# Second layer's norm: squares added a tile later, scaled tiles between the last updates, and the queries' operand in tiles of its own

## The chip, the cores and the metric

The program runs on one core of a Trainium2 chip. TensorE (PE) multiplies, VectorE (DVE), ScalarE (ACT) and GpSimd (POOL) work elementwise, SyncE (SP) issues the DMAs. Each has a queue of its own that runs in order; they meet through semaphores. The metric is device time in microseconds, the median of the runs.

## The reference

Two blocks on x of 1024 positions by 1024 features, in f32. The change lies in the second block, between its pooling layer and its windowed attention:

```python
x = x + gate * pool_mixer(...)               # x, the last product of the pooling layer
# keys and values, one head pair group
hk = modulate(rmsnorm(x, kv_norm_g), shift, scale);  kv = hk @ w_kv          # 1024 x 256
# queries and gates of the attention layer
h = modulate(rmsnorm(x, norm_g[1]), shift1, scale1); q, z = split(h @ w_in)  # 1024 x 2048
# then scores in a band of 128, softmax with sinks, values, silu(z), w_out, a last norm
def rmsnorm(x, g): return x * rsqrt(mean(x * x, axis=-1) + 1e-6) * g
```

Both norms need the same mean of squares of the finished x, with other gains and shifts.

## The kernel before

Everything is held transposed, features on partitions: x is eight tiles X0 to X7 of 128 features by 1024 positions, cut in two halves of 512 positions (h = 0, 1). Each f32 product is three fp32r matmuls of 512 columns (high by high, high by low, low by high), so a unit of 128 output features and one half costs 8 tiles times 3 = 24 matmuls. Operand tiles are `bh` (high) and `bl` (low); weights arrive by DMA in three raw tiles, ScalarE rounds them to `wh`, GpSimd subtracts to `wl`, each unit in two blocks, with six block slots.

The stage `keys` runs thus:

- TensorE makes the last product `pl` of the pooling layer, for h = 0 and then h = 1, tile by tile (12 matmuls each). VectorE adds each into X (`dve_update`), ScalarE squares the updated tile, and VectorE adds the square to an accumulator (`add_square`) right behind the update, so it waits for the square.
- When tile 7 of a half is added, `pe_sums` (eight small matmuls in the trace) sums over partitions, VectorE and ScalarE make the reciprocal root, VectorE spreads it on a diagonal, `pe_rstd` multiplies it out and ScalarE copies it as R (`act_rstd`).
- A pass scales the eight X tiles of one half: VectorE computes `tmp = X * g * R`, ScalarE adds the shift and writes `bh` (for odd tiles in two instructions), and the low part `bl` is made by VectorE for even tiles and by GpSimd for odd ones. Passes in order: 0 (keys, half 0), 1 (keys, half 1), 2 (queries, half 0), 3 (queries, half 1). Passes 2 and 3 write over the tiles of passes 0 and 1, so they wait for v2's product of that half. The scratch `tmp` has three halves (`sc`).
- Pass 0 stands behind the update of tile 2 of half 1; tiles 3 to 7 of half 1 are updated behind it.
- TensorE: k2 and v2 (keys and values) on half 0, then on half 1 (`pe_first_two`; sums of half 1 within k2 behind tile 5, rstd within v2 behind tile 1), then b0 and b1 (the first two of 16 units of queries and gates) likewise, then b2 to b15, both halves at once.
- ScalarE: pass 1, pass 2, then the copies of k2's result out of PSUM (kx0, kx1), of v2's (vt), weights of b1 and b2, then pass 3.
- SyncE: weight loads, the copy of kx between partitions, weight loads, the eight stores of X, then the stores of the queries.

PSUM is four tiles of two halves. `take` gives a wide request the tile whose halves were taken longest ago and a narrow one the half taken longest ago, and makes TensorE wait until the last owner is freed; k2's owner mark is freed by the copy kx1, v2's by vt.

In the attention `sp_window` loads the queries of head pair j; for j = 1 it first waits for `QZ`, the last product of b15.

The lines touched: `dve_scaled`, `act_scaled`, `pool_scaled` (L852 to L915), `dve_update` (L2060), `pe_keys` to `pool_keys` (L2831 to L3055), `sp_window` (L3119). The profile names helper lines: L67 is any matmul, L73 any ScalarE instruction, L76 and L79 VectorE and GpSimd instructions.

Of the kernel before, what the change touches and what calls it, by code (L numbers as in the profile page):

```python
# [133 lines left out]
class Norm:  # L134


    def __init__(self, name, X, acc, R, sq, dg, sc, acc2=None, g1=None, direct=False):
        self.direct = direct
        self.name, self.X, self.acc, self.R, self.acc2, self.g1 = name, X, acc, R, acc2, g1
        self.sq, self.dg, self.sc = sq, dg, sc  # L140
        self.two = g1 is not None
        self.passes = 0


class Net:
# [36 lines left out]
    def setup(self):  # L182
# [70 lines left out]
        self.bl = [m(f"bl{j}", 24 + j, FR) for j in range(NT)]  # L253
        gtile = [32, 33, 34, 35, 0, 1, 2, 3, 4, 5, 6, 7]
# [14 lines left out]
        self.kx0, self.kx1, self.vt = m("kx0", 4), m("kx1", 33), m("vt", 34)  # L269
# [4 lines left out]
        self.T2 = [m(f"t2{i}", 2 * i, cols=2048) for i in range(2)]  # L274
        self.pt2 = [(m(f"p2h{i}", 16 + i, FR), m(f"p2l{i}", 18 + i, FR)) for i in range(2)]
        self.qb = [(m(f"q2h{i}", (5, 20)[i], FR), m(f"q2l{i}", (6, 21)[i], FR)) for i in range(2)]
        otile = [24, 25, 26, 27, 28, 29, 30, 4, 31, 32, 35, 22, 23, 7, 33, 34]
# [3 lines left out]
        self.Y = [m(f"Y{j}", 16 + j if j < 6 else j - 6) for j in range(NT)]  # L281
# [19 lines left out]
        self.n4 = five("n4", self.X)  # L301
# [543 lines left out]
    def sc_place(self, nm, p, j):  # L845
        return 8 * p + j
# [5 lines left out]
    def dve_scaled(self, e, nm, p, h, g, lo, hi, shift=None, after=(), turned=False, hooks={}):  # L852

        c = slice(h * 512, h * 512 + 512)
        r = (nm.acc2 if nm.two else nm.R)[:, c]
        for j in range(NT + 1):
            if j < NT:
                i = self.sc_place(nm, p, j)
                s = nm.sc[i % len(nm.sc)]
                e.wait_ge(*self.at("r", nm.name, h, 1 if nm.two else 0))  # L860
                if i >= len(nm.sc):
                    e.wait_ge(*self.at("scfree", nm.name, i - len(nm.sc)))
                marks = [("scaled", nm.name, p, h, j)]
                if turned:
                    e.wait_ge(*self.at("copied", h, j))
                    marks.append(("free", ("xt", h, j)))
                x = self.ps(("xt", h, j)) if turned else nm.X[j][:, c]
                e.scalar_tensor_tensor(out=s, in0=x, scalar=g(j), in1=r, op0=ALU.mult, op1=ALU.mult).then_inc(
                    self.sig["vec"].up(*marks), 1)
            k = j - 1  # L870
            if k >= 0 and k % 2 == 0:
                i = self.sc_place(nm, p, k)
                s = nm.sc[i % len(nm.sc)]
                for event in after:
                    e.wait_ge(*self.at(*event))
                e.wait_ge(*self.at("scaled", nm.name, p, h, k))
                e.wait_ge(*self.at("nhi", nm.name, p, h, k))
                marks = ("nlo", nm.name, p, h, k), ("scfree", nm.name, i)
                if shift is None:
                    e.tensor_tensor(lo[k][:, c], s, hi[k][:, c].bitcast(F32), ALU.subtract).then_inc(  # L880
                        self.sig["vlo"].up(*marks), 1)
                else:
                    e.scalar_tensor_tensor(out=lo[k][:, c], in0=s, scalar=shift(k), in1=hi[k][:, c].bitcast(F32),
                                           op0=ALU.add, op1=ALU.subtract).then_inc(self.sig["vlo"].up(*marks), 1)
            if j in hooks:
                hooks[j]()

    def act_scaled(self, e, nm, p, h, hi, shift=None, after=(), hooks={}):
        c = slice(h * 512, h * 512 + 512)
        for j in range(NT):  # L890
            s = nm.sc[self.sc_place(nm, p, j) % len(nm.sc)]
            e.wait_ge(*self.at("scaled", nm.name, p, h, j))
            done = self.sig["ahi"].up
            if shift is not None and j % 2:
                e.activation(s, s, ACT.Identity, bias=shift(j)).then_inc(
                    self.sig["evac"].up(("shifted", nm.name, p, h, j)), 1)
                e.wait_ge(*self.at("shifted", nm.name, p, h, j))
            for event in after:
# [5 lines left out]
            if j in hooks:  # L904
                hooks[j]()

    def pool_scaled(self, e, nm, p, h, lo, hi, hooks={}):
        c = slice(h * 512, h * 512 + 512)
        for j in range(1, NT, 2):
# [1150 lines left out]
    def dve_update(self, e, nm, name, h, j, before, gate=None):  # L2060
# [12 lines left out]
        if not nm.two:  # L2073
            self.dve_square(e, nm, j, h)
# [756 lines left out]
    def pe_keys(self, e):  # L2831
        acts = self.made(*zip(*(self.GA[t] for t in range(12, 16))),
                         [[("ghi", "pool", t), ("glo", "pool", t)] for t in range(12, 16)])
        W = self.A["a_w_out_2"][0]
        self.pe_by_halves(e, "pl", lambda j: self.w8(W, 128 * j, 256, k0=1536, nk=4), acts, 4, 256,
                          {1: lambda: self.pe_sums(e, self.n4, 0), 2: lambda: self.pe_rstd(e, self.n4, 0)})
        self.pe_first_two(e, ("k2", "v2"), [self.w8(self.A["w_kv_2"], 128 * i) for i in range(2)], self.bh, self.bl,
                          self.n4, (0, 1))
        Wb = self.A["b_w_in_2"][0]
        self.pe_first_two(e, (("b", 0), ("b", 1)), [self.w8(Wb, 128 * i) for i in range(2)], self.bh, self.bl, self.n4,  # L2840
                          (2, 3), rstd=False)
        h = self.by_norm(self.n4, self.bh, self.bl, (2, 3))
# [7 lines left out]

    POOLED = ("prod", ("pool", 2, 7))
    POOL_OUT = ("prod", ("pl", 1, 7), 1)

    def sp_keys(self, e):
# [3 lines left out]
        e.wait_ge(*self.at("kx", 1))  # L2858
        e.dma_start(self.kx0[64:128, :], self.kx0[0:64, :]).then_inc(self.sig["kx0"].up(("kxt", 0)), 16)
        e.dma_start(self.kx1[0:64, :], self.kx1[64:128, :]).then_inc(self.sig["kx1"].up(("kxt", 1)), 16)  # L2860
        self.sp_w(e, ("b", 0))
        self.sp_w(e, ("b", 1))
        for j in range(NT):
            for h in (0, 1):
                e.wait_ge(*self.at("sum", "n4", h, j))
            e.dma_start(self.xs[j * 128:j * 128 + 128, :], self.X[j][:, :]).then_inc(
                self.sig[f"xs{j}"].up(("xs", j)), 16)
        for j in range(16):
            if j == 3:
                e.wait_ge(*self.at("gst"))  # L2870
                e.wait_ge(*self.at(*self.POOL_OUT))
# [34 lines left out]
    def act_keys(self, e):  # L2906
# [3 lines left out]
        def second():  # L2910
            self.act_rstd(e, self.n4, 0)
            self.act_scaled(e, self.n4, 0, 0, self.bh, self.md(48), [self.POOLED])

        self.half_units(e, "pl", 256, self.act_w,
                        lambda h, j: self.act_square(e, self.n4, j, h, ("sum", "n4", h, j)),
                        {1: lambda: self.act_sums(e, self.n4, 0), 2: second})
        self.act_w(e, "k2", 4)
        self.act_w(e, "v2", 4)
        self.act_sums(e, self.n4, 1)
        self.act_rstd(e, self.n4, 1)  # L2920
        self.act_scaled(e, self.n4, 1, 1, self.bh, self.md(48), [self.POOLED])
        self.act_scaled(e, self.n4, 2, 0, self.bh, self.md(24), [("prod", "v2", 0)])
        e.wait_ge(*self.at("prod", "k2"))
        e.wait_ge(*self.at(*self.POOL_OUT))
# [3 lines left out]
        e.wait_ge(*self.at("prod", "v2"))  # L2928
        e.activation(self.vt[:, :], self.ps("v2"), ACT.Copy).then_inc(self.sig["evac"].up(("vt",), ("free", "v2")), 1)
        self.act_w(e, ("b", 0), 4)  # L2930
        self.act_w(e, ("b", 1), 4)
        self.act_scaled(e, self.n4, 3, 1, self.bh, self.md(24), [("prod", "v2")])
# [60 lines left out]
    def dve_keys(self, e):  # L2993
        for event in self.POOL_TMP:
            e.wait_ge(*self.at(*event))
        self.half_units(e, "pl", 256, None,
                        lambda h, j: self.dve_update(e, self.n4, "pl", h, j, [("px", j, 2)], self.md(16)), {
            1: lambda: self.dve_sums(e, self.n4, 0),
            2: lambda: self.dve_scaled(e, self.n4, 0, 0, self.g3(2), self.bl, self.bh, self.md(48), [self.POOLED])})
        self.dve_sums(e, self.n4, 1)  # L3000
        self.dve_scaled(e, self.n4, 1, 1, self.g3(2), self.bl, self.bh, self.md(48), [self.POOLED])
        self.dve_scaled(e, self.n4, 2, 0, self.g3(1), self.bl, self.bh, self.md(24), [("prod", "v2", 0)])
        self.dve_scaled(e, self.n4, 3, 1, self.g3(1), self.bl, self.bh, self.md(24), [("prod", "v2")])
# [19 lines left out]
    def pool_keys(self, e):  # L3023
# [7 lines left out]
        self.pool_scaled(e, self.n4, 2, 0, self.bl, self.bh)  # L3031
        self.pool_w(e, ("b", 0), 4)
        self.pool_w(e, ("b", 1), 4)
        self.pool_scaled(e, self.n4, 3, 1, self.bl, self.bh)
# [84 lines left out]
    def sp_window(self, e):  # L3119
# [10 lines left out]
        def fetch(n):  # L3130
# [6 lines left out]
            if j == 1:  # L3137
                e.wait_ge(*self.at(*self.QZ))
            else:
# [381 lines left out]
```

## Time and profile before

| | us |
|---|---|
| median of 3 runs | 2616.27 (2615.64 to 2618.62) |
| the profiled execution, its time | 2616.37 |
| its span | 2614.1 |
| TensorE busy | 2491.4 (95%) |
| VectorE busy | 1665.0 (64%) |
| ScalarE, GpSimd busy | 950.2, 658.7 |

Times in the trace count from the span's start. The stage of the change lies between about 2095 and 2220 us, the units b2 to b15 run to 2380 us, the windowed attention to about 2505 us. The granted clock of TensorE over the span is 0.986.

### The profile page before, as it was taken

To read this page: it belongs to the slowest core of one execution; us is meant where nothing else is said; L and a number is where in the kernel's file an instruction comes from. 1 tells how busy PE (TensorE), PEld (TensorE's weight loads), DVE (VectorE), ACT (ScalarE), POOL (GpSimd) and SP (SyncE) were. 2 spreads that over 40 slices of the span, in tenths; PEclk is the share of its full clock that TensorE was granted. 3 is DMA by queue.
4 is the path that set the end of the run, shared out by engine and by line. 5 is a ranking of instruction groups with operands and counts; after the bars stand their busy time and mean duration, and the time that the engine had idled before them with its cause. 6 is when DMAs were issued, how large, how long until landed. Compare 5 with 4: busy or idle time off the path is not lost.

```text
span 2614.1 us, 32078 instructions
## 1 busy us (share of the span) xinstructions
PE 2491.4 (95%) x12208; PEld 2052.8 (79%) x12208; DVE 1665.0 (64%) x2829; ACT 950.2 (36%) x1764; POOL 658.7 (25%) x536
## 2 busy tenths in 40 slices
PE   7899999888999899999999999999999998999998
PEld 5688888777887688888888877888877775888987
DVE  4699999476425877786644368476595566104843
ACT  5521212577123422222312244233243245225842
POOL 3167322576443000000000120000000044334753
PEclk9999999999999999999999999999999999999999
DMA  5112333001354365564623132232355123533242
GB/s 187 33 41 65 97 97 112 26 1 67 127 189 125 105 199 188 171 188 141 231 75 113 61 109 81 97 97 89 105 201 217 43 70 113 177 118 104 102 159 100
DMA packets 264323, 302.10 MB, mean 116 GB/s; under 512 B 11272, under 2 KB 216556, under 8 KB 264172
## 3 DMA queue, kind: packets, MB, share of 16 engines
q1 hardware_dynamic: 263860, 299.96, 35.1%
q8 instruction: 99, 1.62, 0.3%
q14 instruction: 52, 0.43, 0.1%
q10 hardware_dynamic: 312, 0.09, 0.0%
HBM read 228.15 MB, written 70.29 MB: 114 GB/s over the span
## 4 chain that ended last, share of the span: by engine, by line
PE 83%; DVE 10%; ACT 4%; issue 1%; DMA 1%; POOL 1%; SPq 0%; DVEq 0%; ACTq 0%; POOLq 0%
PE ps L67 81%; PE ps L70 2%; DVE tmp L79 1%; DVE sm L79 1%; ACT tmp L73 1%; DVE tmp L76 1%; ACT pth L73 1%; DVE wl L76 1%; DVE X L79 1%; DVE pwa L76 1%; DVE B2l L76 1%; DVE ptl L79 0%; DVE bl L79 0%; DVE pwb L76 0%; DVE ws L76 0%
## 5 line engine op out<-in xcount | busy, mean ns | idle before, releaser
L76 POOL TENSOR_TENSOR wl<-raw,wh 128x512 fp32r<-128x512 f32 (+1 forms) x224 | 293.4, 1330 | 1568.6 <-ACT wh L73 1568.4
L73 ACT ACTIVATE wh<-raw 128x512 fp32r<-128x512 f32 (+1 forms) x388 | 226.4, 621 | 243.6 <-PE ps L67 183.3
L67 PE MATMUL ps<-B2h,wh 128*128 128x512 f32 x616 | 244.1, 396 | 13.5 <-DVE B2l L76 7.0
L67 PE MATMUL ps<-B2l,wh 128*128 128x512 f32 x616 | 241.3, 392 | 0.0
L67 PE MATMUL ps<-B2h,wl 128*128 128x512 f32 x616 | 241.1, 391 | 0.0
L73 ACT ACTIVATE tmp<-ps 128x512 f32<-128x512 f32 (+5 forms) x163 | 118.2, 736 | 325.2 <-PE ps L67 313.9
L76 DVE TENSOR_TENSOR tmp<-tmp,ps 128x512 f32<-128x512 f32 x204 | 138.4, 685 | 109.0 <-PE ps L67 92.7
L67 PE MATMUL ps<-ah,wh 128*128 128x512 f32 (+1 forms) x608 | 192.5, 393 | 9.2 <-DVE al L76 5.0
L73 ACT ACTIVATE wh<-ws 128x512 fp32r<-128x512 f32 x152 | 94.3, 626 | 291.4 <-DVE ws L76 263.9
L67 PE MATMUL ps<-B3h,wh 128*128 128x512 f32 x448 | 178.3, 398 | 15.2 <-DVE B3l L76 7.1
L67 PE MATMUL ps<-ah,wl 128*128 128x512 f32 (+1 forms) x608 | 190.4, 390 | 0.0
L67 PE MATMUL ps<-al,wh 128*128 128x512 f32 (+1 forms) x608 | 190.3, 390 | 0.0
L67 PE MATMUL ps<-B3l,wh 128*128 128x512 f32 x448 | 176.0, 393 | 0.0
L67 PE MATMUL ps<-B3h,wl 128*128 128x512 f32 x448 | 176.0, 393 | 0.0
L100 DVE MATCH_REPLACE8 sm<-m,sm 128x384 f32<-128x384 f32 (+2 forms) x192 | 167.9, 889 | 0.0
L97 DVE MAX8 m<-sm 128x8 f32<-128x384 f32 (+2 forms) x192 | 162.2, 893 | 0.0
L67 PEld LDWEIGHTS ps<-B2h,wh 128*128 128x128 f32 x616 | 116.4, 189 | 43.2 <-issue 8.0
L76 DVE TENSOR_TENSOR X<-X,ps 128x1024 f32<-128x1024 f32 (+1 forms) x56 | 59.6, 1068 | 132.1 <-PE ps L67 132.1
L67 PEld LDWEIGHTS ps<-ah,wh 128*128 128x128 f32 (+1 forms) x608 | 113.3, 187 | 36.5 <-issue 10.7
L67 PEld LDWEIGHTS ps<-B2h,wl 128*128 128x128 f32 x616 | 116.6, 189 | 24.8
L67 PEld LDWEIGHTS ps<-B2l,wh 128*128 128x128 f32 x616 | 116.7, 189 | 23.6 <-issue 0.2
L67 PEld LDWEIGHTS ps<-ah,wl 128*128 128x128 f32 (+1 forms) x608 | 113.6, 187 | 24.7 <-issue 0.2
(292 smaller groups left out, 5751.7 us busy)
## 6 DMA issues: line engine op xcount, KB each, us to landing
ada<-in_ada_w SPq DMA_DIRECT2D x48, 512.0 KB, 3.7
raw<-in_w_in SPq DMA_DIRECT2D x37, 512.0 KB, 4.4
raw<-in_a_w_in SPq DMA_DIRECT2D x33, 512.0 KB, 4.6
gates<-tmp SPq DMA_DIRECT2D x32, 512.0 KB, 3.0
raw<-in_w_ffn_gate SPq DMA_DIRECT2D x24, 512.0 KB, 5.9
hd<-tmp SPq DMA_DIRECT2D x22, 512.0 KB, 4.6
gf<-hd SPq DMA_DIRECT2D x22, 512.0 KB, 7.2
raw<-in_a_w_out SPq DMA_DIRECT2D x20, 512.0 KB, 3.4
```

Of the source, the lines that this page charges most:

```text
L67: return self.e.matmul(*a, **k) if self.e else Ins()
L70: return self.e.transpose(*a, **k) if self.e else Ins()
L73: return self.e.activation(*a, **k) if self.e else Ins()
L76: return self.e.tensor_tensor(*a, **k) if self.e else Ins()
L79: return self.e.scalar_tensor_tensor(*a, **k) if self.e else Ins()
L97: return self.e.max(*a, **k) if self.e else Ins()
L100: return self.e.match_replace(*a, **k) if self.e else Ins()
```

## The change

1. Squares of half 1 are added a tile later: `update(j)`, then the square of tile j - 1. The sums of half 0 are made behind `pl`'s tile 0 and the rstd behind tile 1 (before: 1 and 2). Pass 0 begins earlier, and the updates of tiles 2 to 6 stand between its scaled tiles.
2. The operand of passes 2 and 3 gets tiles of its own (`bh2`, `bl2`): six of each are free when `pl` is done, and only the last two, which lie on `bh0` to `bh3`, wait for v2's product of that half. Tiles 0 to 3 of pass 2 are made before pass 1, the rest behind it. A fourth scratch half comes in.
3. k2 and v2 on half 0: the sums of half 1 come within v2, behind its tile 0, and the rstd behind its tile 4.
4. ScalarE copies kx0, kx1 and vt behind pass 3, the weights of b2 behind them. SyncE stores X before it loads the weights of b3 and b4 and copies kx. Tables, kx, vt, the second pair of query tiles, o2 and Y change places, and the wait for `QZ` goes.

```diff
+    self.bh2 = [m(f"bh2{j}", i, FR) for j, i in enumerate((4, 5, 6, 7, 0, 1, 16, 17))]
+    self.bl2 = [m(f"bl2{j}", i, FR) for j, i in enumerate((32, 33, 34, 35, 2, 3, 18, 19))]
...
+    self.n4 = Norm("n4", self.X, t[0], t[1], half(t[2]), half(t[3])[:1], half(t[3])[1:] + half(t[4]) + half(t[0])[:1],
+                   order=[(p, j) for p, n in ((0, range(8)), (2, range(4)), (1, range(8)), (2, range(4, 8)), (3, range(8))) for j in n])
...                                                                            # pe_keys
-                          {1: lambda: self.pe_sums(e, self.n4, 0), 2: lambda: self.pe_rstd(e, self.n4, 0)})
-        self.pe_first_two(e, ("k2", "v2"), ...)
+                          {0: lambda: self.pe_sums(e, n4, 0), 1: lambda: self.pe_rstd(e, n4, 0)})
+        self.pe_halves_of_two(e, ("k2", "v2"), ...,
+                              ({}, {0: lambda: self.pe_sums(e, n4, 1), 4: lambda: self.pe_rstd(e, n4, 1)}))
...
+    def pe_halves_of_two(self, e, keys, w8s, acts, hooks=({}, {})):
+        us = [self.unit(k, w) for k, w in zip(keys, w8s)]
+        for i in range(2):
+            self.gemm(e, keys[i], us[i], acts, (0,), hooks=hooks[i], end=False)
+        for i in range(2):
+            self.gemm(e, keys[i], us[i], acts, (1,))
+    def b_place_free(self, h):
+        return lambda j: [self.POOL_OUT] if j < 6 else [("prod", "v2", 0), ("prod", "v2")][h:h + 1]
...                                                                            # act_keys
+        self.act_scaled(e, n4, 0, 0, self.bh, self.md(48), [self.POOLED],
+                        hooks={0: square(2), 2: square(3), 3: four, 5: square(5), 7: six})
+        sq1(1, 7)
+        b0 = self.act_steps(e, n4, 2, 0, self.bh2, self.md(24), tiles=self.b_place_free(0))
+        next(b0)
+        self.act_sums(e, n4, 1)
+        for j in range(1, 4):
+            next(b0)
+        self.act_rstd(e, n4, 1)
+        self.act_w(e, "v2", 4)
+        self.act_scaled(e, n4, 1, 1, self.bh, self.md(48), [self.POOLED])
+        for j in b0:
+            pass
+        self.act_w(e, ("b", 0), 4)
+        self.act_scaled(e, n4, 3, 1, self.bh2, self.md(24), tiles=self.b_place_free(1))
+        e.wait_ge(*self.at("prod", "v2"))
         ... kx0, kx1 (frees k2), vt (frees v2)
         self.act_w(e, ("b", 1), 4)
...                                                                            # dve_keys
+        def second(j):
+            update(1, j, False)
+            if j > 1:
+                self.dve_square(e, n4, j - 1, 1)
+        second(0)
+        self.dve_sums(e, n4, 0)
+        second(1)
+        self.dve_scaled(e, n4, 0, 0, self.g3(2), self.bl, self.bh, self.md(48), [self.POOLED],
+                        hooks={0: later(2), 2: later(3), 3: later(4), 5: later(5), 7: later(6)})
+        second(7)
...                                                                            # pool_keys
         self.pool_w(e, "k2", 4)
+        self.pool_scaled(e, self.n4, 2, 0, self.bl2, self.bh2, tiles=range(4))
         self.pool_w(e, "v2", 4)
         self.pool_scaled(e, self.n4, 1, 1, self.bl, self.bh)
+        self.pool_scaled(e, self.n4, 2, 0, self.bl2, self.bh2, tiles=range(4, 8))
         self.pool_w(e, ("b", 0), 4)
+        self.pool_scaled(e, self.n4, 3, 1, self.bl2, self.bh2)
         self.pool_w(e, ("b", 1), 4)
...                                                                            # sp_window
-            if j == 1:
-                e.wait_ge(*self.at(*self.QZ))
-            else:
+            if j > 1:
                 e.wait_ge(*self.at("prod", ("s2", 4 * j - 5)))
```

GpSimd makes pass 0's low parts before the weights of k2 and v2, in both versions.

## Rows read from the trace of the kernel before

**Rows 1.** The page, part 4: shares of the chain that ended last.

```profile
PE 83%; DVE 10%; ACT 4%; issue 1%; DMA 1%; POOL 1%; SPq 0%; DVEq 0%; ACTq 0%; POOLq 0%
```

**Rows 2.** Stretches: length, busy PE, PEld, DVE, ACT, POOL, granted clock, DMA share, GB/s.

```profile
2151.00:2155.00 4.00, 3.39 (x8) 2.77 (x9) 2.82 (x4) 1.73 (x4) 1.53 (x3) 0.50 0.29 81
...
2220.00:2300.00 80.00, 80.00 (x340) 63.60 (x339) 8.57 (x7) 20.98 (x28) 27.75 (x20) 1.00 0.50 165
```

**Rows 3.** TensorE in order: start us, us, operation, idle before and its releaser.

```profile
2129.10 0.95 PE L67 MATMUL ps<-ones,tmp 128*128 128x1 f32 x8
...
2133.22 1.13 PE L67 MATMUL ps<-tmp,ones 128*128 128x512 f32 x2 [0.29 <-DVE tmp L76]
...
2151.61 0.77 PE L67 MATMUL ps<-bh,wh 128*128 128x512 f32 x1 [3.62 <-ACT tmp L73]
...
2160.12 1.36 PE L67 MATMUL ps<-ones,tmp 128*128 128x1 f32 x8 [1.49 <-DVE tmp L76]
...
2198.68 0.77 PE L67 MATMUL ps<-bh,wh 128*128 128x512 f32 x1 [2.25 <-POOL wl L76]
...
2213.98 0.47 PE L67 MATMUL ps<-bh,wh 128*128 128x512 f32 x1 [1.16 <-POOL bl L76]
...
2220.18 0.62 PE L67 MATMUL ps<-bh,wh 128*128 128x512 f32 x2
```

**Rows 4.** VectorE's waits, 2129 to 2214 us: in total, times, longest.

```profile
DVE bl L79 <- ACT bh L73: 7.0, 10, 5.3
DVE tmp L79 <- ACT tmp L73: 5.8, 1, 5.8
DVE tmp L76 <- ACT tmp L73: 4.9, 7, 0.7
```

**Rows 5.** VectorE in order, columns as in rows 3.

```profile
2134.53 1.57 DVE L76 TENSOR_TENSOR tmp<-tmp,tmp 128x512 f32<-128x512 f32 x1 [0.70 <-ACT tmp L73]
...
2168.76 1.42 DVE L79 SCALAR_TENSOR_TENSOR tmp<-X,gs,tmp 128x512 f32<-128x512 f32 x2 [5.78 <-ACT tmp L73]
...
2175.70 1.47 DVE L79 SCALAR_TENSOR_TENSOR bl<-tmp,mod,bh 128x512 fp32r<-128x512 f32 x1 [0.20 <-ACT bh L73]
...
2180.41 2.45 DVE L79 SCALAR_TENSOR_TENSOR tmp<-X,gs,tmp 128x512 f32<-128x512 f32 x2
...
2192.83 1.40 DVE L79 SCALAR_TENSOR_TENSOR tmp<-X,gs,tmp 128x512 f32<-128x512 f32 x2
```

**Rows 6.** ScalarE in order, columns as in rows 3.

```profile
2168.12 0.60 ACT L73 ACTIVATE tmp<-ps 128x512 f32<-128x512 f32 x1 [6.21 <-PE ps L67]
...
2193.57 2.04 ACT L73 ACTIVATE kx<-ps 64x1024 f32<-64x1024 f32 x2
...
2211.86 0.63 ACT L73 ACTIVATE bh<-tmp 128x512 fp32r<-128x512 f32 x1
```

**Rows 7.** GpSimd in order, columns as in rows 3.

```profile
2149.68 2.79 POOL L76 TENSOR_TENSOR wl<-raw,wh 128x512 fp32r<-128x512 f32 x2
...
2159.93 2.50 POOL L76 TENSOR_TENSOR wl<-raw,wh 128x512 fp32r<-128x512 f32 x2 [2.47 <-ACT wh L73]
...
2175.01 1.61 POOL L76 TENSOR_TENSOR bl<-tmp,bh 128x512 fp32r<-128x512 f32 x1 [2.05 <-ACT bh L73]
...
2197.26 5.89 POOL L76 TENSOR_TENSOR wl<-raw,wh 128x512 fp32r<-128x512 f32 x4 [1.91 <-ACT wh L73]
```

**Rows 8.** SyncE and TensorE in order, around the stores of x and the attention's start.

```profile
2200.26 7.99 SPq L109 DMA_DIRECT2D xs<-X  x8
...
2379.84 0.61 PE L67 MATMUL ps<-bh,wl 128*128 128x512 f32 x2
...
2381.54 0.32 SPq L109 DMA_DIRECT2D qd<-tmp  x1
...
2382.44 0.66 SPq L109 DMA_DIRECT2D q2h<-qd  x1
...
2389.10 0.33 PE L67 MATMUL ps<-k2h,q2h 64*128 64x128 f32 x2 [3.39 <-DMA q2l<-qd]
```

More of the change, by code:

```diff
@@ L845, in sc_place, with dve_scaled, dve_steps @@
     def sc_place(self, nm, p, j):
-        return 8 * p + j
+        return nm.order.index((p, j)) if nm.order else 8 * p + j
     def lows(self, p, j, shift):
         return "plo" if j % 2 else "vlo"
-    def dve_scaled(self, e, nm, p, h, g, lo, hi, shift=None, after=(), turned=False, hooks={}):
+    def dve_scaled(self, *a, hooks={}, **k):
+        for j in self.dve_steps(*a, **k):
+            if j in hooks:
+                hooks[j]()
+    def dve_steps(self, e, nm, p, h, g, lo, hi, shift=None, after=(), turned=False, tiles=None):
         c = slice(h * 512, h * 512 + 512)
@@ L873, in dve_scaled @@
                 s = nm.sc[i % len(nm.sc)]
-                for event in after:
+                for event in tiles(k) if tiles else after:
                     e.wait_ge(*self.at(*event))
@@ L884, in dve_scaled, with act_scaled, act_steps @@
                                            op0=ALU.add, op1=ALU.subtract).then_inc(self.sig["vlo"].up(*marks), 1)
+            yield j
+    def act_scaled(self, *a, hooks={}, **k):
+        for j in self.act_steps(*a, **k):
             if j in hooks:
                 hooks[j]()
-    def act_scaled(self, e, nm, p, h, hi, shift=None, after=(), hooks={}):
+    def act_steps(self, e, nm, p, h, hi, shift=None, after=(), tiles=None):
         c = slice(h * 512, h * 512 + 512)
@@ L897, in act_scaled @@
                 e.wait_ge(*self.at("shifted", nm.name, p, h, j))
-            for event in after:
+            for event in tiles(j) if tiles else after:
                 e.wait_ge(*self.at(*event))
@@ L2072, in dve_update @@
                                    op1=ALU.add).then_inc(self.sig["vec"].up(*marks), 1)
-        if not nm.two:
+        if not nm.two and squares:
             self.dve_square(e, nm, j, h)
@@ L2995, in dve_keys @@
             e.wait_ge(*self.at(*event))
[L2996 to L3003, printed above, removed]
+        n4 = self.n4
+        update = lambda h, j, squares=True: self.dve_update(e, n4, "pl", h, j, [("px", j, 2)], self.md(16), squares=squares)
+        def second(j):
+            update(1, j, False)
+            if j > 1:
+                self.dve_square(e, n4, j - 1, 1)
+        later = lambda j: lambda: second(j)
+        for j in range(NT):
+            update(0, j)
+        second(0)
[4 more added lines that the diff above has]
+        second(7)
+        b0 = self.dve_steps(e, n4, 2, 0, self.g3(1), self.bl2, self.bh2, self.md(24), tiles=self.b_place_free(0))
+        next(b0)
+        self.dve_square(e, n4, 7, 1)
+        next(b0)
+        self.dve_sums(e, n4, 1)
+        for j in range(2, 4):
+            next(b0)
+        self.dve_scaled(e, n4, 1, 1, self.g3(2), self.bl, self.bh, self.md(48), [self.POOLED])
+        for j in b0:
+            pass
+        self.dve_scaled(e, n4, 3, 1, self.g3(1), self.bl2, self.bh2, self.md(24), tiles=self.b_place_free(1))
         for j in range(NT):
```

85 lines of the change are left out of this document (43 added, 42 removed).

## The prediction

> **What bounds the kernel now.** I read the chain that ended last first: TensorE holds 83% of it, VectorE 10% and ScalarE 4% [rows 1]. A change that only moves norm work can therefore win no more than the places where that chain leaves TensorE. Next I cut the stretch of the diff by time. From 2220 us to the start of the windowed attention TensorE is busy without a gap at the full clock [rows 2], so whatever the stage gains or loses by the end of unit b1 is handed on unchanged, and the ruler is the first matmul of unit b2, at 2220.18 us [rows 3]. Between 2148 and 2220 us TensorE stands still before k2 (3.62 us), before the second sums (1.49), before b1 (2.25) and tile by tile in between, and after the first it runs at the 1.2 GHz level for a while (granted clock 0.50) [rows 2, 3].
>
> VectorE's waits say why [rows 4]: 4.9 us for ScalarE's squares (0.7 each), 5.8 us for the copied rstd of the second half, 7.0 us for ScalarE's high parts, of which 5.3 is one wait, while ScalarE copied kx and vt [rows 6]. That is 17.7 us of idle VectorE in front of a stage that VectorE paces: eight scaled tiles take 11.65 and 12.42 us (first scaled tile at 2168.76, 2180.41, 2192.83) [rows 5], while the 48 matmuls that they feed take 10.9.
>
> Passes 0 and 1 are the keys' operand of half 0 and 1, passes 2 and 3 the queries'. One VectorE instruction costs 0.67 us (two start within 1.42) [rows 5]. One matmul costs 0.227 at the full clock (27 from 2213.98 to 2220.18, the first a little longer) and 0.43 at half (8 in 3.39) [rows 2, 3].
>
> **Window stage: nothing.** The diff drops SyncE's wait for the last product of b before it loads the second pair of queries. TensorE does lose 3.39 us there, for that very load. But SyncE stores b15's tile first, at 2381.54, which itself comes after that product's last matmul (2379.84), and issues the load at 2382.44 [rows 8]. The removed wait had been met over a microsecond earlier and the queue order is unchanged: gain 0. Bounds: 0, and 3.39 if the load did go out earlier. The moved tables and kx tiles only rename places, and SyncE's eight stores of x move ahead of the loads of b3's and b4's weights and of the kx copies; I cost them at nothing, since those weights are used only behind b2, over 40 us after the updates of x are done. If that cover were gone, it would cost the 8 us that the stores take on SyncE [rows 8].
>
> **Pass 0 and k2's start: +3.0 us.** The sums of half 0 move ahead by one product of 12 matmuls, 2.72 us, from 2129.10, and the rstd matmul from 2133.22 to about 2130.5 [rows 3]. With ScalarE's copy behind a square, R is there near 2132.2. But now VectorE adds one update and one square between the scaled tiles. From the product of tile 2 (2130.5 + 0.6 + 2.72 = 2133.8) to the last scaled tile stand 18 instructions, 12.1 us, and GpSimd's operations among them hold up four at about 1 us: the square's addition of 1.57 at 2134.53 instead of 0.69, the low part of 1.47 at 2175.70 beside GpSimd's 1.61 at 2175.01 [rows 5, 7]. The last scaled tile is then ready at 2149.9, about 3 us later than without the updates between. Behind it ScalarE shifts and copies (1.4), GpSimd makes that tile's low part (1.5) and only then, in its order, k2's first weight block (1.5, the pair at 2149.68 took 2.79 [rows 7]), and 0.4 later TensorE starts: 2154.7 against 2151.61 [rows 3] (whose row names the square that ended last; by the times it is this weight block), taken as +3.0. The stall that should go grows to 7 us, because GpSimd's queue was not reordered. Bounds: 0 (nothing held) and +4.
>
> **The second half's rstd: +1.5 us.** k2's first half is 24 matmuls, 13 of them at the low clock as now: 8.1 us, to 2162.7. Then v2's first tile (0.7), the sums (1.0; the eight small matmuls took 0.95 at 2129.10 and 1.36 at 2160.12 [rows 3]), mean, root, reciprocal and diagonal (1.5): 2165.9. TensorE no longer limits: ScalarE's copy of R now stands behind pass 2's tiles 1 to 3, of which tile 3 can be scaled only after the diagonal, once at 0.67 and once held at 1.7, then 1.4 to shift and copy and 0.6 for R itself: 2170.2, against 2168.72 before [rows 6]. VectorE still waits about 4 us for these sums. Bounds: -1 and +3.
>
> **Twenty tiles instead of twenty-four.** Behind R come pass 1 (8 tiles), the last 4 of pass 2 and pass 3 (8); only 4 tiles have moved ahead, and the 5.3 us wait is gone. Eight tiles are 12.0 us on the mean of the two rows, or 12.7 up to ScalarE's last copy (for pass 2 13.2, from 2180.41 to kx's copy at 2193.57, which is 0.7 more than its 12.42 [rows 5, 6]). But the low parts of b0, which GpSimd made at 2159.93 while VectorE stood idle [rows 5, 7], now fall into pass 1, and those of b1 into pass 3: four more held instructions, 4.0 us. With 0.5 for b1's high parts in ScalarE's queue: 2170.2 + 12.0 + 2.0 + 6.0 + 12.7 + 2.0 + 0.5 = 2205.4 for ScalarE's last copy, which was 2212.49 [rows 6]. So the norm ends 7.1 us earlier. Bounds of the four: 0 and 1.7 each (the four at 2197.26 took 5.89 us and beside them VectorE's instructions came every 1.74 [rows 7]).
>
> The Trainium skill, "SBUF — State Buffer", Who interferes with whom, says that a VectorE instruction with two SBUF inputs and a GpSimd instruction that reads SBUF shut each other out completely, and that one with a PSUM input goes free. By that rule additions of squares and scaled tiles are the held kind and the updates are not, and four full operations of GpSimd at their mean of 1.4 us would make 5.6 of my 4.0 and the time 2623.8 us; the row at 2175.70 shows half to two thirds of an operation, so the sum stays with it.
>
> **What the earlier end is worth: the new wait.** TensorE's tail was short: the last tile of pass 3 is wanted late, in b0's second half, and only 27 matmuls follow (6.2 us). In the changed kernel b1's first half is behind another event. PSUM tiles are given to the one whose halves were taken longest ago. With the new order of takes (sums 0 before product 1; k2, v2, sums 1, b0, b1), b1 again gets k2's tile, since sums 1 now comes later than k2. That tile is free when ScalarE has copied kx1. Before, the copies stood ahead of pass 3 (2193.57, two of 1.02 [rows 6]) and b1 started at 2198.68 for GpSimd's weights [rows 3]. Now they stand behind it. Queued behind the waiting b1 are b0's second half and b1's own. So b1 starts at 2205.4 + 2.0 + 0.3 = 2207.7, after b0's first half has ended near 2199 (pass 1 done near 2184, v2's half and b0's half 5.4 each, from k2's last tile, with its gaps: 2188 + 10.9): TensorE stands for over 8 us. Then 72 matmuls follow, 16.3 us, the first ten at 0.43 as in the rows after a standstill (2.0 more; bounds 1.3 and 2.6): 2226.0. Against 2220.18 this is +5.8 us.
>
> **Sum.** The profiled execution took 2616.37 us with a span of 2614.1, 0.1 above the median of 2616.27, so both serve as base: 2616.4 + 5.8 = 2622.2 us. In parts, against before: up to the second R +1.5 (k2 starts 3.0 later, and the 1.49 standstill before its sums is gone); from R to ScalarE's last copy 35.2 us instead of 43.8, -8.6 (four tiles ahead -6.0, the one wait -5.3, held instructions and b1's high parts +4.5, and -1.8 for the crowd of held instructions that now follows that wait); from the last copy to b2 20.6 us instead of 7.7, +12.9.
>
> **Rivals.**
> A, the wait exists but decides less. The held instructions don't add up (0 instead of 4.0) and k2 starts at 2151.61: b1 starts at 2207.7 - 4.0 - 3.0 = 2200.7, the time is 2615.2. For it: 18 instructions that wait for nothing would leave GpSimd gaps. Against: rows 5 show three to four held of every twelve.
> B, the other side: b1 gets a tile that is free, and starts right behind b0. Then the stage ends by TensorE's own work or by pass 3's last tile: 2205.4 + 1.5 + 6.2 = 2213.1, -7.1 us, 2609.3 us. It decides if sums 1 is taken before v2 or if b0's tile is the later one; the order of takes in the diff speaks against it, the 17.7 us of idle VectorE for a gain as such.
> C, the removed wait of SyncE does release the load: 3.4 us less, 2618.8. Rows 8 speak against it.
> D, the norm is later than summed (second rstd after 2173, every block of weights held fully): b1 at 2212, 2627 us.
>
> **How the numbers follow.** Forecast 0.62 (2619 to 2626), A 0.16, B 0.10, C 0.04, D 0.08. About 0.2%, 5.2 us, is what a measurement tells from no change. The forecast lies just beyond it, so of its 0.62 some 0.44 is slower and 0.18 within; D is slower; A and C are within; of B 0.08 is faster and 0.02 within. Slower 0.53, same 0.39, faster 0.08. The range is 2615 to 2627: B is left out, and the two bounds of the held instructions and of k2's start (about -6 and +5 on the forecast) are in.
>
> **What would show it.** In the changed profile: k2's first matmul after an idle stretch of 6 to 8 us, with GpSimd's weights as releaser; the copy of the second R near 2170; a wait of TensorE of 6 to 9 us before b1, ended by ScalarE's kx copy (the surest sign); VectorE's wait for squares gone; pass 3's last copy on ScalarE near 2205; the 3.39 us wait for the second queries still there. The prediction is wrong if b1 starts right behind b0, or if b2 starts before 2218 us.

## The result, and the profile after

| | before | after |
|---|---|---|
| median of 6 runs each, us | 2616.11 (2614.26 to 2618.62) | 2626.14 (2623.30 to 2627.87) |
| the profiled execution, its span | 2614.1 | 2625.6 |

The changed kernel takes 1.0037 of the time before, 95% interval 1.0024 to 1.0050. A second series beside other kernels gave 1.0025 (1.0015 to 1.0035), 2624.52 against 2618.63 us. So it is slower by 6 to 10 us; forecast were 2622.2 (+5.8), with 2615 to 2627 as the range.

**How far apart the two traces stand where.** Below, the stage is counted from its own entry, the first 512-column update of X's second half: 2126.58 us before, 2131.41 after.

| from the entry, us | before | after | difference | forecast |
|---|---|---|---|---|
| k2's first matmul | 25.03 | 28.33 | +3.30 | +3.0 |
| second copy of R | 41.54 | 43.24 | +1.70 | +1.5 |
| ScalarE's last copy of pass 3 ends | 85.91 | 79.36 | -6.55 | -7.1 |
| b2's first matmul | 93.60 | 99.59 | +5.99 | +5.8 |
| b15's store, the end of the stage | 254.96 | 260.97 | +6.01 | +5.8 |

From that store to the end of the span it is 232.6 and 233.2 us. The other 4.83 us of the difference between the two spans lie ahead of the entry, where the kernels are alike; experiment 9 is about them. A "low clock" below is the 1.2 GHz level of TensorE.

TensorE in order in the changed kernel, as [rows 3]:

```profile
2131.21 0.95 PE L67 MATMUL ps<-ones,tmp 128*128 128x1 f32 x8
...
2135.34 1.12 PE L67 MATMUL ps<-tmp,ones 128*128 128x512 f32 x2 [0.29 <-DVE tmp L76]
...
2159.74 0.76 PE L67 MATMUL ps<-bh,wh 128*128 128x512 f32 x1 [6.91 <-POOL wl L76]
...
2168.64 0.95 PE L67 MATMUL ps<-ones,tmp 128*128 128x1 f32 x8
...
2180.14 0.77 PE L67 MATMUL ps<-bh,wh 128*128 128x512 f32 x1 [4.71 <-DVE bl L79]
...
2212.78 0.80 PE L67 MATMUL ps<-bh,wh 128*128 128x512 f32 x1 [8.86 <-ACT kx L73]
...
2231.00 0.62 PE L67 MATMUL ps<-bh,wh 128*128 128x512 f32 x2
```

Three stalls have taken the place of the old ones. The first, before k2, grew from 3.62 to 6.91 us and now names GpSimd's low weights. The second, 4.71 us ahead of the second halves of k2 and v2, is new: there TensorE waits for pass 1's first tile, which VectorE can only begin when it has the second R. The third, before b1, is new too: 8.86 us, ended by ScalarE's kx copy. The standstill before the second sums (1.49 in [rows 3]) is gone. The prediction speaks of the first and the third. The second costs nothing in this kernel, since b1 waits for the kx copy whatever TensorE does before; it counts once b1 has a tile of its own (experiment 8).

ScalarE in order, as [rows 6]: the second R, the last copy of pass 3, and right behind it the two kx copies.

```profile
2174.65 0.58 ACT L73 ACTIVATE tmp<-ps 128x512 f32<-128x512 f32 x1
...
2210.14 0.63 ACT L73 ACTIVATE bh<-tmp 128x512 fp32r<-128x512 f32 x1
2210.68 2.04 ACT L73 ACTIVATE kx<-ps 64x1024 f32<-64x1024 f32 x2
```

The pair of kx copies ends at 2212.72 and b1 starts at 2212.78. Before, the pair began at 2193.57, ahead of pass 3.

VectorE's waits from 2134 to 2220 us, as [rows 4], and VectorE in order, as [rows 5]:

```profile
DVE r L82 <- PE ps L67: 4.6, 1, 4.6
DVE bl L79 <- ACT bh L73: 2.6, 8, 1.2
DVE tmp L79 <- ACT tmp L73: 2.5, 2, 1.3
```

```profile
2158.18 1.74 DVE L79 SCALAR_TENSOR_TENSOR tmp<-X,gs,tmp 128x512 f32<-128x512 f32 x1
2159.85 1.76 DVE L76 TENSOR_TENSOR tmp<-tmp,tmp 128x512 f32<-128x512 f32 x1
...
2169.62 0.16 DVE L82 TENSOR_SCALAR r<-ps 128x4 f32<-128x4 f32 x1 [4.64 <-PE ps L67]
...
2198.20 1.76 DVE L79 SCALAR_TENSOR_TENSOR bl<-tmp,mod,bh 128x512 fp32r<-128x512 f32 x1 [1.19 <-ACT bh L73]
2199.89 3.48 DVE L79 SCALAR_TENSOR_TENSOR tmp<-X,gs,tmp 128x512 f32<-128x512 f32 x2
```

The wait for squares (4.9 us in [rows 4]) and the 5.3 us behind the kx copies are no longer there. What the change set out to remove is removed, and VectorE is through earlier by 6 to 7 us. GpSimd in order, as [rows 7]:

```profile
2155.87 1.84 POOL L76 TENSOR_TENSOR bl<-tmp,bh 128x512 fp32r<-128x512 f32 x1 [2.70 <-ACT bh L73]
2157.68 6.76 POOL L76 TENSOR_TENSOR wl<-raw,wh 128x512 fp32r<-128x512 f32 x4
...
2198.12 2.99 POOL L76 TENSOR_TENSOR wl<-raw,wh 128x512 fp32r<-128x512 f32 x2
```

The weights of k2, and v2's behind them (four blocks in all), begin the moment GpSimd is through with pass 0's last low part. The instructions of VectorE at 2158.18, 2159.85, 2198.20 and 2199.89 lie beside GpSimd's weights, the last of them in part beside the low part that follows, and take 1.74 to 1.76 us each.

Stretches of the changed kernel, columns as in [rows 2]:

```profile
2212.80:2217.00 4.20, 4.20 (x11) 3.35 (x12) 0.00 (x0) 2.01 (x3) 2.52 (x2) 0.54 0.49 125
2217.00:2227.00 10.00, 10.00 (x46) 8.29 (x45) 0.18 (x1) 1.03 (x1) 0.00 (x0) 1.00 0.00 0
2235.00:2300.00 65.00, 65.00 (x281) 52.44 (x280) 6.12 (x5) 12.55 (x18) 19.44 (x15) 1.00 0.52 166
```

Behind the standstill the granted clock is 0.54 for 4.2 us (the 1.2 GHz level for 3.9 of them) and then full again. From b2 on TensorE has no gap, as before: from b2's first matmul to b15's store it is 161.4 us in both kernels. So the delay is handed on unchanged.

### The profile page after: what moved, and what is told of

Read it like the earlier page. It is cut to its first block, busy times and chain, and to the rows that moved or that the text cites. A ratio compares the mean times of both kernels' runs of the same rounds, so it can differ in the third digit from the quotient of the medians.

```text
span 2625.6 us, 32075 instructions
## 1 busy us (share of the span) xinstructions
PE 2496.1 (95%) x12208; PEld 2059.0 (78%) x12208; DVE 1666.7 (63%) x2829; ACT 949.6 (36%) x1764; POOL 661.0 (25%) x536
## 4 chain that ended last, share of the span: by engine, by line
PE 84%; DVE 9%; ACT 3%; issue 1%; DMA 1%; POOL 1%; SPq 0%; DVEq 0%; ACTq 0%; POOLq 0%
PE ps L67 81%; PE ps L70 3%; DVE tmp L79 1%; DVE sm L79 1%; ACT tmp L73 1%; DVE tmp L76 1%; ACT pth L73 1%; DVE wl L76 1%; DVE pwa L76 1%; DVE B2l L76 1%; DVE X L79 1%; DVE ptl L79 0%; DVE pwb L76 0%; DVE XO L79 0%; DVE bl L79 0%
```

## The experiments

Each stage length below runs from the entry to b15's store, from one profiled execution. In the two kernels that were traced more than once it repeats within 0.06 us (before 254.96 and 255.00; changed 260.97, 261.03 and 261.02). That is not the whole of its scatter. Where TensorE's clock rises some matmuls sooner or later, kernels whose instructions are the same up to the second R have it at different times: 43.24 to 43.28 us from the entry in three traces of the changed kernel, but 41.89 in experiment 1 and 43.49 in experiment 7; 41.54 and 41.56 in the kernel before, but 39.96 in experiment 4; 37.67 in experiment 2, but 38.90 in experiment 3. So a difference of stages is good to a tenth only where R stands at the same time in both, and otherwise to 1 to 3 us. Medians are coarser still.

| kernel | median, us (runs) | ratio to before, 95% | stage, us |
|---|---|---|---|
| changed, again | 2624.52 (8) | 1.0025, 1.0015 to 1.0035 | 261.03 |
| 1 another tile for b1 | 2613.85 (11) | 0.9983, 0.9975 to 0.9992 | 247.20 |
| 2 k2's low weights earlier | 2620.29 (11) | 1.0008, 0.9999 to 1.0017 | 256.40 |
| 3 both | 2607.64 (6) | 0.9964, 0.9952 to 0.9976 | 243.81 |
| 4 before, kx copied late | 2625.93 (4) | 1.0034, 1.0021 to 1.0048 | 261.42 |
| 5 updates behind pass 0 | 2620.85 (10) | 1.0010, 1.0000 to 1.0019 | 257.76 |
| 6 b0's weights earlier | 2621.40 (11) | 1.0013, 1.0004 to 1.0022 | 257.81 |
| 7 queries loaded together | 2623.40 (9) | 1.0020, 1.0011 to 1.0030 | 261.34 |
| 8 the best of them | 2605.52 (5) | 0.9954, 0.9940 to 0.9968 | 243.99 |

The kernel before had medians of 2617.6 to 2618.6 beside them (13 to 25 runs).

**The changed kernel again**, unedited.

> The changed kernel once more, as the base of this group. In its first trace the first update of half 1 (the entry of the stage) started 4.8 us later than in the kernel before, and unit b2 10.8 us later, so 6.0 us belong to the stage and 4.8 us lie ahead of it, where nothing was changed. Theory (the entry shift is chance of one execution): the median is 6 to 8 us above before, and this trace's entry lies elsewhere than at +4.8. Rival (the shift ahead of the stage is a property of the changed program): entry again at +4 to +5 and the median at +10 to +11.

The stage repeats. The entry is late again, at 2130.97 us (+4.4), which was the rival's sign; the median is 5.9 above the kernel before, which was nearer the theory's. Experiment 9 decides it.

**1. Another PSUM tile for b1.** The rule of `take` is made to see k2's and v2's tiles as just taken:

```diff
         h = self.by_norm(n4, self.bh2, self.bl2, (2, 3))
+        for key in ("k2", "v2"):
+            for half in self.halves:
+                if half.before == [key]:
+                    half.taken = self.takes + 0.5
```

> Changed kernel, but k2's and v2's PSUM tiles count as taken later, so that b1 gets the tile of the last product of pl and sums 1, free since the second R. Theory (TensorE's 8.9 us before b1 is the wait for k2's tile): the wait is gone, b1 starts right behind b0's first half, b2 about 10.7 us earlier counted from the entry (8.9 and the low clock behind it), time 10 to 11 us under the changed kernel, about that of before. Rival (the norm bounds the stage anyway, the wait only hides it): b0's second half then waits for pass 3's last tiles and the gain is under 5 us.

TensorE's waits from 2129 to 2240 us in this kernel (us in total, times, longest); the one for kx is gone and none has taken its place:

```profile
PE ps L67 <- POOL wl L76: 6.9, 1, 6.9
PE ps L67 <- DVE bl L79: 5.4, 3, 4.7
PE ps L67 <- POOL bl L76: 2.0, 2, 1.5
```

13.8 us less by the stage, where 10.7 were expected (by the medians it is 10.7): 8.86 of wait and 1.9 of low clock behind it are the expected part. The other 3 us come from places ahead of b1: TensorE's clock rises sooner there, though no instruction differs. The stretch behind the second R, in the changed kernel and in this one:

```profile
2180.00:2193.00 13.00, 11.49 (x25) 7.63 (x26) 12.41 (x13) 7.97 (x12) 5.35 (x4) 0.51 0.13 40
```

```profile
2179.00:2192.00 13.00, 10.12 (x32) 6.64 (x33) 12.40 (x13) 7.97 (x12) 5.33 (x4) 0.83 0.15 41
```

Clock 0.51 with 25 matmuls against 0.83 with 32. Already within k2 it rose 31.0 us from the entry instead of 34.0. By the time b1 can start this has made 3.0 us (69.5 from the entry instead of 72.5). Why is open, and so 3 of the 13.8 us can't be credited to the edit. The cause of the wait, k2's tile, is shown.

**2. k2's low weights behind pass 0's tile 3** on GpSimd:

```diff
-                        {2: lambda: self.pool_scaled(e, self.n4, 0, 0, self.bl, self.bh)})
+                        {2: lambda: self.pool_scaled(e, self.n4, 0, 0, self.bl, self.bh,
+                                                     {3: lambda: self.pool_w(e, ("pl", "w", 1, 4))})})
```

> Changed kernel, but GpSimd makes k2's low weights behind pass 0's tile 3 instead of behind tile 7. Theory (k2's start is held by GpSimd's order): k2 starts within 1 us of pl's end instead of 6.9 us behind it, runs into pass 0's last tile near 2157.7 (times as in the first trace), ends about 8 us earlier, the second R comes 4 to 6 us earlier, and since b1 waits for kx behind pass 3 the gain at b2 is the same 4 to 6 us. Rival (the second R is bound by VectorE's squares, whose last addition ended at 2161.6): R moves under 3 us and so does b2.

k2 starts at 21.25 instead of 28.33 and the second R comes 5.6 us earlier. TensorE's waits:

```profile
PE ps L67 <- ACT kx L73: 10.3, 1, 10.3
...
PE ps L67 <- POOL wl L76: 0.8, 1, 0.8
```

In front of k2 nothing of the 6.9 us is left: it starts right behind `pl`. The 0.8 is in front of v2, for v2's own weights. Two smaller waits are new, 1.45 us for pass 0's last low part and 1.30 for the last addition of squares, so that of k2's 7.1 us R keeps 5.6. The copy of kx and with it b1 come 5.6 us earlier as well, which is what VectorE's chain wins. The wait for kx still grew from 8.9 to 10.3, since TensorE is there 7.1 us earlier and the copy only 5.6. The stage wins 4.6: behind this wait 14 matmuls ran at the low clock instead of 9, which takes 1 us back.

**3. Both.** 

> Both edits, of b1's tile and of k2's low weights. Theory (two separate waits in series): the gains add up, 14 to 17 us under the changed kernel, 2609 to 2612 us. Rival (without the wait for the tile TensorE's own work from v2 on bounds the stage): the second edit then adds under 3 us to the first, 2613 to 2616 us.

Stage 17.2 us under the changed kernel's, where the two alone make 18.4; by the medians 16.9. That is the theory's side, but not by much: to experiment 1's stage the second edit adds 3.4 us, where the rival allowed 3. And the sum can't be tested closely: 3 of experiment 1's 13.8 us are the clock's, and here the second R comes 1.2 us later than in experiment 2 with the same instructions ahead. The kernel beats the one before by 11.0 us.

**4. The kernel before with the kx and vt copies behind pass 3** (on ScalarE; the weights of b2, high parts on ScalarE and low parts on GpSimd, likewise behind it):

```diff
+        self.act_w(e, ("b", 0), 4)
+        self.act_scaled(e, self.n4, 3, 1, self.bh, self.md(24), [("prod", "v2")])
         e.wait_ge(*self.at("prod", "k2"))
         ... kx0, kx1, vt
-        self.act_w(e, ("b", 0), 4)
         self.act_w(e, ("b", 1), 4)
-        self.act_scaled(e, self.n4, 3, 1, self.bh, self.md(24), [("prod", "v2")])
```

> Kernel before, with one thing of the change alone: ScalarE copies kx and vt behind pass 3 instead of ahead of it, and b2's weights behind them. Theory (the place of the copies decides, since b1 takes k2's tile): TensorE waits some 10 us before b1 with kx's copy as releaser; VectorE's 5.3 us wait shrinks to about 1 us, so pass 3 ends 4 us earlier, near 2208.5, b1 starts near 2211 and b2 near 2229: 8 to 10 us over before. Rival (pass 3 ends so much earlier that the wait costs nothing): within 2 us of before.

This move, in a kernel with nothing else of the change, costs 6.4 us of stage (255.00 to 261.42) and 0.34% of the time, 8.4 us by the medians. VectorE's wait of 5.3 us shrank to 1.2, as expected. The stage had been put at 8 to 10 us, and the miss lies ahead of the edit: the second R came 1.6 us earlier than in the kernel before (39.96 us from the entry, not 41.54), since 8 matmuls ran at the low clock behind the second sums instead of 12. With R in its old place the move would cost about 8 us (an estimate, 6.4 + 1.6). The wait before b1 shows itself with the same releaser:

```profile
PE ps L67 <- ACT kx L73: 13.5, 1, 13.5
```

**5. The updates of tiles 3 to 7 behind pass 0**, and ScalarE's squares likewise; their squares are still added a tile later:

```diff
-        self.dve_scaled(e, n4, 0, 0, self.g3(2), self.bl, self.bh, self.md(48), [self.POOLED],
-                        hooks={0: later(2), 2: later(3), 3: later(4), 5: later(5), 7: later(6)})
-        second(7)
+        second(2)
+        self.dve_scaled(e, n4, 0, 0, self.g3(2), self.bl, self.bh, self.md(48), [self.POOLED])
+        for j in range(3, 8):
+            second(j)
```

> Changed kernel, but the updates of tiles 3 to 7 and their squares stand behind pass 0 again, not between its tiles; squares still a tile later, GpSimd's order as changed. Theory (the interleaved updates push out tile 7 of pass 0, and with it k2's weights on GpSimd): k2 starts 21.5 to 23 us behind the entry instead of 28.3, the second R comes 4 to 6 us earlier, b2 likewise, 5 us under the changed kernel. Rival (the weights are late for another reason, ScalarE's order or the DMA): k2's start stays within 1 us of 28.3.

k2 starts at 25.43, waits 4.0 us for the weights instead of 6.9, and the stage is 3.3 us shorter. I had expected 21.5 to 23 for k2 and was wrong: pass 0 by itself takes 11.7 us (2137.99 to 2149.71), and 4.4 more go on its last low part and the first block of weights. So the updates between the tiles cost 2.9 of the 3.3 us by which k2 is later than in the kernel before. R came 3.1 us earlier, where 4 to 6 were expected. VectorE beside those weights, in this kernel (the next two instructions are the same again):

```profile
2154.24 0.74 DVE L79 SCALAR_TENSOR_TENSOR X<-ps,mod,X 128x512 f32<-128x512 f32 x1
2154.90 1.11 DVE L76 TENSOR_TENSOR tmp<-tmp,tmp 128x512 f32<-128x512 f32 x1
```

The update, with one input in PSUM, takes its 0.74; the addition of squares, with both in SBUF, takes 1.1 instead of 0.68.

**6. b0's weights split ahead of pass 2's first tiles**, while VectorE waits for the sums:

```diff
         sq1(1, 7)
+        self.act_w(e, "v2", 4)
         b0 = self.act_steps(e, n4, 2, 0, ...)
...
         self.pool_w(e, "k2", 4)
+        self.pool_w(e, "v2", 4)
         self.pool_scaled(e, self.n4, 2, 0, self.bl2, self.bh2, tiles=range(4))
-        self.pool_w(e, "v2", 4)
```

> Changed kernel, but b0's weights are split by ScalarE and GpSimd ahead of pass 2's tiles, in the 4.6 us in which VectorE waits for the second sums, instead of beside pass 1. Theory (each of GpSimd's operations beside pass 1 holds one VectorE instruction for about 1 us): from the second R to ScalarE's last copy 33.5 us instead of 35.5, b2 2 us earlier plus up to 0.6 for the shorter way to R. Rival (held instructions are hidden by VectorE's own waits for ScalarE): that stretch stays within 0.5 us of 35.5.

The second R stands at 43.24 us from the entry, as without the edit; from there to the kx copies it is 33.1 us instead of 36.0, and the stage is 3.2 us shorter. By the first scaled tile of each pass, 1.7 of the 2.9 us are saved in pass 1, where the weights stood (12.25 us instead of 13.99), which is the part that held instructions explain; the forecast had 2.0 for it. The other 1.2 are saved behind it, most of them in pass 3, where VectorE's wait of 1.19 us for ScalarE is gone. The edit moves ScalarE's part of the weights too, so this part can't be put down to GpSimd.

**7. The second pair of queries loaded with the first**, ahead of b10's weights:

```diff
             if j == 10:
                 self.sp_queries(e, 0)
+                self.sp_queries(e, 1)
...
-            self.sp_queries(e, j)                        # for each j
+                self.sp_queries(e, j)                    # for j > 1 alone
```

> The changed kernel, but the second pair of queries is loaded together with the first, ahead of the stores that close the queries, so that the load really leaves its place (the changed kernel only dropped the wait in front of it). Theory of the prediction (rival C fell since the load is issued where it was, behind the stores): the 3.8 us wait of TensorE at the start of the windowed attention, in which it stands for the second pair, goes; the stage up to b15's store stays at 261.0 us, and the time is 3.0 to 3.8 us under the changed kernel's, about 2621.5. Rival: the wait is VectorE's (the trace of the changed kernel names its state tile st as the releaser), then it stays at 3.8 us, and the time is the changed kernel's, about 2625.

TensorE at that place, in experiment 9's trace of the changed kernel and in this one:

```profile
2395.76 0.48 PE L67 MATMUL ps<-k2h,q2h 64*128 64x128 f32 x2 [3.60 <-DMA q2l<-qd]
```

```profile
2394.31 0.47 PE L67 MATMUL ps<-k2h,q2h 64*128 64x128 f32 x2 [1.32 <-DVE st L103]
```

Both theories were half right. The load was what ended the wait, but right behind it stood VectorE: of 3.6 us 2.3 go. From b15's store to the end of the span it is 232.0 us, here and in experiment 8, instead of 233.1. The eleven traces without this edit have between 232.6 and 234.5 us there, so what the edit wins at the end is not clear of scatter, and the medians, 1.1 us apart, can't tell it from nothing either. The stage, in which nothing was edited that TensorE waits for, is 0.3 us longer than the changed kernel's.

**8. Edits 1, 2, 6 and 7 together.** 

> The changed kernel with four edits together: b1 takes another PSUM tile than k2's; k2's low weights are made behind pass 0's tile 3; b0's weights are split ahead of pass 2's first tiles; the second pair of queries is loaded with the first. If what each brought in its own run adds up: stage -13.8 (tile), -4.6 less 1.2 that the pair was short of the sum (weights), -3.2 (b0's weights), and -3.4 at the attention, together -23.8 on 2624.5, about 2601 us. Rival: with the tile freed TensorE's work is the bound of the stage between k2 and b2, and b0's weights, which only hurried ScalarE's copies behind pass 3, bring nothing more: stage -17.2, about 2604 us. The stage from its entry to b15's store is 240.6 us by the first and 243.8 by the second.

The rival had it. The stage is as long as with edits 1 and 2 alone (243.99 and 243.81): the kx copies come 1.8 us earlier by edit 6, and b1's result comes no earlier (82.83 and 82.65 from the entry), since with a tile of its own b1 no longer waits for them. The two traces differ in clock too: between k2 and b2 18 matmuls ran at the low level here and 14 in experiment 3, so up to 1 us of edit 6 may be hidden by that. TensorE's waits from 2125 to 2240 us are down to 10.5 us, from 22.2 in the changed kernel:

```profile
PE ps L67 <- DVE bl L79: 4.2, 1, 4.2
PE ps L67 <- POOL bl L76: 3.3, 4, 1.4
PE ps L67 <- DVE tmp L76: 2.2, 3, 1.3
PE ps L67 <- POOL wl L76: 0.8, 1, 0.8
```

The longest that is left, 4.2 us, is the one for pass 1's first tile, which was hidden before.

At 2605.52 us this is the fastest kernel here, 12.4 us under the kernel before (2617.88 beside it) and 18 to 21 under the changed one (2623.36 in the same series, one run; 2624.52 and 2626.14 in the others).

**9. Where the stage begins.** 

> The changed kernel once more, for one look at where its profiled execution stands when the stage begins. In two profiled executions it stood at 2131.4 and 2131.0 us, the kernel before at 2126.6 and 2128.2, though no instruction ahead of that point differs in kind. If that is chance of the execution, this one may stand anywhere between 2126.5 and 2132; if it belongs to the changed kernel, it stands at 2131 again. The stage itself should again be 261.0 us long.

The third trace of the changed kernel has its entry at 2126.99, within 0.5 us of the kernel before in its first trace, and takes 2623.36 us, 1.2 from the forecast; its stage is 261.02. A second trace of the kernel before:

> The kernel before once more, for a second trace. Theory (where the stage is entered is chance of one execution, stages are not): entry anywhere between 2126 and 2132 us, from the entry to b15's store 255.0 us again within 0.7. Rival (the changed program is slower ahead of the stage): entry at 2126 to 2127 again.

It had its entry at 2128.21 and a stage of 255.00. So the 4.83 us ahead of the stage are no work of the change; they scatter with the execution. The other kernels say the same: the six others that hold the change without experiment 1's late 2131.75 stand at 2127.31 to 2128.70. Part of the shift shows in the clock of the stretch from 500 to 600 us; changed kernel with its entry at 2131.41, and at 2126.99:

```profile
500.00:600.00 100.00, 86.79 (x684) 0.93 0.01 1
```

```profile
500.00:600.00 100.00, 86.73 (x701) 0.96 0.01 1
```

The late one has the lower clock there and 17 matmul records fewer. The other late trace had 0.95 there, but so had experiment 8's, whose entry is early (2127.31), so this stretch is a part of it and not all. Set side by side, instruction by instruction, VectorE of the late trace is behind the early one's by 0.2 us at 500 us, 2.9 at 900 and 4.5 at 1010, and from there to the entry it stays between 4.4 and 4.6. The other late trace is behind by 0.3, 2.3 and 4.0. So the shift is made between 500 and 1010 us, over a thousand us ahead of the change; from 900 to 1000 us both late traces have a clock of 0.98 and the early one 1.00. That is not the whole either: the first trace of the kernel before has 0.98 there too, and has made it up again by 1720 us.

## Why the prediction was right

The sign and the mechanism were right, and so was the size of the stage. By the steps of the prediction:

- **Window stage, nothing:** right. The wait is still there (3.6 to 3.8 us), and the load is issued where it was, behind b15's store; rival C is out. Its upper bound of 3.39 was too high even so: experiment 7 frees the load and gets 2.3 at the wait, and at the end no more than scatter. The moved tables, stores and loads cost nothing either, as put: b2's first matmul to b15's store takes 161.4 us before and after.
- **Pass 0 and k2's start, +3.0:** measured +3.30. It came by the cause named, GpSimd's weights in order behind pass 0's last low part; experiments 2 and 5 split it into queue order and updates. Held instructions were the squares' additions and scaled tiles; each update took its 0.74. Two small misses offset each other: held instructions ahead of the last scaled tile cost 3.0 us, not 4, and that tile was ready 0.4 us sooner than summed; GpSimd's low part and first weight block behind it took 1.84 and about 1.7 us, not 1.5 each.
- **The second rstd, +1.5:** measured +1.70 in three traces of the changed kernel. With the same instructions it stood at +0.35 in experiment 1 and at +1.95 in experiment 7, so that it is met within 0.2 is in part chance.
- **Twenty tiles instead of twenty-four:** 35.2 us were summed from R to the last copy, 35.5 measured (2175.23 to 2210.77). The parts agree as well. VectorE in the changed kernel, first scaled tiles of pass 1, of pass 2's tile 4 and of pass 3:

```profile
2175.26 3.06 DVE L79 SCALAR_TENSOR_TENSOR tmp<-X,gs,tmp 128x512 f32<-128x512 f32 x2 [1.28 <-ACT tmp L73]
...
2189.25 2.42 DVE L79 SCALAR_TENSOR_TENSOR tmp<-X,gs,tmp 128x512 f32<-128x512 f32 x2
...
2195.61 1.40 DVE L79 SCALAR_TENSOR_TENSOR tmp<-X,gs,tmp 128x512 f32<-128x512 f32 x2
```

  That is 14.0 us (forecast 12.0 + 2.0), 6.4 (6.0) and, up to 2210.77, 15.2 (12.7 + 2.0 + 0.5). Rival A had the held instructions add nothing; taking one of the two blocks away (experiment 6) brought 1.7 us in the pass where it stood, of 2.0 summed, so they do.
- **The new wait:** b1 was put at 81.1 us from the entry and stands at 81.37; the wait at over 8 and is 8.86; from there to b2 18.3 and is 18.22, of it 1.9 by the low clock. That k2's PSUM tile is the cause is shown twice: giving b1 another takes the wait away (experiment 1), and moving its release behind pass 3 in the kernel before brings the wait and 6.4 us of stage (experiment 4). The stall of 4.71 us ahead of the second halves is in no line of the prediction; it fell inside the time that b1 had to wait anyway. Rival B is out by the order of takes.
- **The measured time:** 2626.14 is 3.9 above the forecast. The stage gives +6.0, the median difference is +10.0 in the first series and +5.9 in the second. The rest is most likely scatter ahead of the stage, some 5 us between traces, which is as wide as what a measurement was said to tell; only one execution of each series was traced, so for the medians this is argued and not shown. That the first median stayed 0.9 us inside the range owes something to luck. The chances as listed add up to slower 0.52, same 0.40, faster 0.08; the prediction writes 0.53 and 0.39.

On the rule of the Trainium skill that the prediction weighed ("SBUF — State Buffer", Who interferes with whom): the trace agrees that an update, with one input in PSUM, is not held (0.74 us in experiment 5 beside GpSimd's weights). An instruction with two inputs in SBUF beside GpSimd's weights took up to 1.77 us where it takes 0.74 alone, 1.0 each, as summed, and not the 1.4 that the rule would make it. Either VectorE ran on in part while GpSimd's operation was under way, or that operation does not hold what they share for all of its recorded time; no run here tells the two apart. For the sum the measurement decides.

What stays open: why the low clock behind k2's start and behind R was shorter in experiment 1, by 3 us when b1 is reached, and behind the second sums in experiment 4, by 1.6, with the same instructions ahead; and what makes the clock differ between 500 and 1010 us, where the entry's scatter comes from.

## What to carry to other kernels

A copy out of PSUM is not only work of ScalarE: it gives a tile back, and the allocator decides who waits for it. When such a copy is moved behind other work, look up who takes that tile next and what is queued behind him; here a norm that ended 6.6 us sooner became 6.0 us of loss, and four lines at the allocator turned it into a gain. When work is put earlier on one engine, look at the engines that follow in order: behind GpSimd's unmoved queue TensorE stood for 7 us, and one moved call took that away. And compare stages from a landmark at their own entry: the same stage repeated within 0.06 us while the whole execution scattered by 5. Check a second landmark inside the stage, ahead of the edit, before believing the tenths: in experiments 1 and 4 it had moved by 1.4 and 1.6 us, and the clock had done it.

## What the runs showed of the hardware

- VectorE and GpSimd, both reading SBUF, came in turn here: beside four blocks of weights on GpSimd (6.76 us, 1.69 each) VectorE's instructions with two SBUF inputs came one for one, 1.74 to 1.77 us each.
- How soon the clock rises again is not a property of the instructions alone: behind k2's first matmul it took 5.7 us in three executions of the changed kernel, 6.1 in experiment 7 and 2.7 in experiment 1, whose instructions up to there are the same.
